# A prologue re-divided between TensorE and VectorE: half of each modulation sum, the transposes' eviction, the identity table's load and the rope angles

## What is computed

```python
cond = jax.nn.silu(c)                                  # 1024 values
mod = cond @ ada_w[i] + ada_b[i]                       # 1024 x 3072 for each layer
shift, scale, gate = jnp.split(mod, 3)
h = rms_norm_f32(x, norm_g[i]) * (1.0 + scale) + shift
out = retention_mixer(h, positions, ...)               # layer 0; q, k, v, g = split(h @ w_in)
x = x + gate * out
...
ang = positions[..., None] * inv_freq                  # in retention_mixer
cos, sin = jnp.cos(ang), jnp.sin(ang)
q = apply_rope(q, cos, sin); k = apply_rope(k, cos, sin) * RET_QK_DIM ** -0.5
```

## Time and profile before

| | |
|---|---|
| median of 3 runs | 2000.1 us (1998.48 to 2002.16) |
| the profiled execution: its time, its span | 1999.29 us, 1997.5 us |
| busy in the span: TensorE, VectorE, GpSimd, ScalarE | 1887.8 us (95%), 820.1 us (41%), 1104.3 us (55%), 458.1 us (23%) |
| mean granted TensorE clock, as a share of full speed | 0.968 |
| first of the projections' matmuls starts | 42.80 us |
| `tok` of tiles 4 and 5 starts | 66.91 us |

### The profile page before, as it was taken

The page is one execution under the profiler, slowest core; times in us unless marked ns, Lnnn a source line. Parts: engine busy times, 40 slices in busy tenths (PEclk is TensorE's granted clock), DMA queues, the critical chain, the costliest instruction groups (busy, mean ns, idle before and its releaser), DMA issues.

```text
span 1997.5 us, 27167 instructions
## 1 busy us (share of the span) xinstructions
PE 1887.8 (95%) x9662; PEld 1557.1 (78%) x9662; DVE 820.1 (41%) x1417; ACT 458.1 (23%) x933; POOL 1104.3 (55%) x856
## 2 busy tenths in 40 slices
PE   8999999998899999999998999989889869999998
PEld 4878888877788888888877778877768558887886
DVE  5642515444333432333322865975342553102300
ACT  3121111100222222222210246435122322001200
POOL 3755546486255444454456558752156468767862
PEclk9999999998899999999999998979899979999999
DMA  9423222265132222222223312110022133333331
GB/s 353 130 68 91 68 72 80 79 238 172 53 86 82 82 69 68 83 83 83 69 74 95 89 48 59 33 32 11 32 74 64 34 93 95 95 95 94 96 95 42
DMA packets 279466, 172.72 MB, mean 86 GB/s; under 512 B 5936, under 2 KB 269936, under 8 KB 278384
## 3 DMA queue, kind: packets, MB, share of 16 engines
q1 hardware_dynamic: 272912, 151.01, 26.0%
q10 hardware_dynamic: 6496, 20.93, 3.1%
HBM read 169.69 MB, written 2.10 MB: 86 GB/s over the span
## 4 chain that ended last, share of the span: by engine, by line
PE 83%; DVE 10%; ACT 2%; issue 2%; DMA 1%; POOL 1%; SPq 0%; DVEq 0%; ACTq 0%; POOLq 0%
PE acc L373 18%; PE acc L375 17%; PE acc L374 17%; PE acc L414 3%; PE acc L415 3%; PE acc L416 3%; PE st L427 3%; PE sc L1387 2%; PE ob L1332 2%; PE sc L1367 2%; DVE ada_acc L2069 2%; PE bc L460 2%; DVE conv_out L2192 2%; PE sc L1295 1%; DVE hn L508 1%
## 5 line engine op out<-in xcount | busy, mean ns | idle before, releaser
L711 POOL TENSOR_TENSOR wl<-raw,wh 128x512 fp32r<-128x512 f32 x464 | 651.8, 1426 | 19.4
L708 POOL TENSOR_SCALAR wh<-raw 128x1024 fp32r<-128x1024 f32 x232 | 258.0, 1112 | 724.0 <-PE acc L375 408.4
L373 PE MATMUL acc<-hh,wh 128*128 128x512 f32 x1056 | 430.5, 408 | 19.8 <-DVE hl L502 6.7
L375 PE MATMUL acc<-hh,wl 128*128 128x512 f32 x1056 | 417.3, 395 | 0.0
L374 PE MATMUL acc<-hl,wh 128*128 128x512 f32 x1056 | 416.5, 394 | 0.0
L373 PEld LDWEIGHTS acc<-hh,wh 128*128 128x128 f32 x1056 | 201.5, 191 | 69.6 <-issue 19.3
L375 PEld LDWEIGHTS acc<-hh,wl 128*128 128x128 f32 x1056 | 201.3, 191 | 43.5
L374 PEld LDWEIGHTS acc<-hl,wh 128*128 128x128 f32 x1056 | 202.2, 192 | 41.5 <-issue 2.2
L373 PE MATMUL acc<-Yh,wh 128*128 128x512 f32 x512 | 203.1, 397 | 5.5 <-DVE xT L577 5.5
L374 PE MATMUL acc<-Yl,wh 128*128 128x512 f32 x512 | 202.3, 395 | 0.0
L375 PE MATMUL acc<-Yh,wl 128*128 128x512 f32 x512 | 202.3, 395 | 0.0
(11 more groups left out here) (401 smaller groups left out, 2809.3 us busy)
## 6 DMA issues: line engine op xcount, KB each, us to landing
raw<-in_att_w_in SPq DMA_DIRECT2D x64, 512.0 KB, 4.0
raw<-in_mlp_w SPq DMA_DIRECT2D x64, 512.0 KB, 4.0
raw<-in_ret_w_in SPq DMA_DIRECT2D x48, 512.0 KB, 3.8
ada_w<-in_ada_w ACTq DMA_DIRECT2D x8, 1536.0 KB, 8.1
raw<-in_w_in SPq DMA_DIRECT2D x23, 512.0 KB, 3.7
ada_w<-in_ada_w SPq DMA_DIRECT2D x16, 512.0 KB, 10.7
raw<-in_ret_w_out SPq DMA_DIRECT2D x16, 512.0 KB, 4.0
raw<-in_att_w_out SPq DMA_DIRECT2D x16, 512.0 KB, 3.9
```

What stands on the lines that cost most here:

```text
L373: e.matmul(bank[:, :], wh[:, s, k, :], rhs_high(k), start=(start and k == 0), stop=False)
L375: last = e.matmul(bank[:, :], wl[:, s, k, :], rhs_high(k), start=False, stop=(stop and k == k1 - 1))
L708: e.tensor_scalar(wh[:, s, :, :], raw[:, s, :, :], 1.0, 1.0, ALU.mult, ALU.mult).then_inc(high_done, 1)
L711: low = e.tensor_tensor(wl[:, s, k0:k0 + KT // 2, :], raw[:, s, k0:k0 + KT // 2, :], wh[:, s, k0:k0 + KT // 2, :].bitcast(F32), ALU.subtract)
```

## The change

Four edits at the entry:

1. **Half of each block on VectorE.** `ada_half(n)` multiplies tiles 0 to 3 of block `n` with their value of `cond` and adds them up in `ada_acc0[:, n % 2, :]` (one TENSOR_SCALAR and three SCALAR_TENSOR_TENSOR over 128x512). TensorE multiplies tiles 4 to 7 as before and adds the partial sum over partitions by one more matmul with `ones`, which waits for `ada_half{n}` and stands in front of tile 6. So 5 matmuls for each block in place of 8.
2. **Transposes evicted by VectorE.** The eight evictions to `xT` move from ScalarE to VectorE as tensor copies.
3. **Identity table first.** The load of `const` moves from the second place of ScalarE's queue to the first of SyncE's, and the load of `pos` behind ScalarE's squares.
4. **Rope angles behind the norm.** The ten VectorE steps that make the angles move from the front of its program to behind the last `low`, ahead of the gate's partial sums; the two sines on ScalarE move behind its eight `hh`.

```diff
+        ada_acc0 = at("ada_acc0", [P, 2, S], W + 16 * KB)
...
+            e.dma_start(const[:, :], ins["const"]).then_inc(const_in, 16)
             for t in range(NT):
                 e.dma_start(x_tok[:, t, :], ins["x"][0, t * P:(t + 1) * P, :]).then_inc(x_in[t], 16)
...
-            e.dma_start(const[:, :], ins["const"]).then_inc(const_in, 16)
-            e.dma_start(pos[:, :], ins["positions"].to_broadcast([P, S])).then_inc(pos_in, 16)
...
-                x_out(t, 0)
-                x_out(t, 1)
+            e.dma_start(pos[:, :], ins["positions"].to_broadcast([P, S])).then_inc(pos_in, 16)
             e.dma_start(dec[:, :], ins["decay"][0]).then_inc(decay_in, 16)
             e.dma_start(glev[:, :, :], ins["levels"].rearrange("p (l n) -> p l n", l=LEVELS)).then_inc(levels_in, 16)
-            e.wait_ge(*V.at("angles"))
-            e.activation(sin_[:, :], ang[:, :], ACT.Sin).then_inc(*AC.done())
-            e.activation(cos_[:, :], tmp[:, 1, :], ACT.Sin).then_inc(*AC.done("rope"))
             e.wait_ge(*V.at("mod02"))
             for k in range(KT):
...
                 e.activation(hh[:, k, :], hn[:, k, :], ACT.Identity, bias=mod[:, 0, 0, k:k + 1]).then_inc(*AC.done(f"n0hi{k}"))
+            e.wait_ge(*V.at("angles"))
+            e.activation(sin_[:, :], ang[:, :], ACT.Sin).then_inc(*AC.done())
+            e.activation(cos_[:, :], tmp[:, 1, :], ACT.Sin).then_inc(*AC.done("rope"))
...
-                for k in range(KT):
+                for k in range(4, KT):
                     if k % 2 == 0:
                         e.wait_ge(ada_in[n][k // 2], 16)
+                    if k == 6:
+                        e.wait_ge(*V.at(f"ada_half{n}"))
+                        e.matmul(sc[n % 2][:, :], ones[:, :], ada_acc0[:, n % 2, :], start=False, stop=False)
                     last = e.matmul(sc[n % 2][:, :], cond[:, 0, k:k + 1].to_broadcast([P, P]), ada_w0[n][:, k, :],
-                                    start=(k == 0), stop=(k == KT - 1))
+                                    start=(k == 4), stop=(k == KT - 1))
...
+            for n in range(2 * NT):
+                e.wait_ge(*PE.at(f"x{n}"))
+                e.tensor_copy(xT[:, 4 * (n % 2):4 * (n % 2) + 4, n // 2 * P:(n // 2 + 1) * P],
+                              ob[n % 2][:, :].rearrange("p (k n) -> p k n", k=4)).then_inc(*V.done(f"x{n}"))
...
+            def ada_half(n):
+                if n >= 2:
+                    e.wait_ge(*PE.at(f"ada{n - 2}"))
+                for k in range(4):
+                    if k % 2 == 0:
+                        e.wait_ge(ada_in[n][k // 2], 16)
+                    x = ada_acc0[:, n % 2, :]
+                    if k == 0:
+                        step(e, e.tensor_scalar(x, ada_w0[n][:, 0, :], cond[:, 0, 0:1], None, ALU.mult), V)
+                    else:
+                        step(e, e.scalar_tensor_tensor(out=x, in0=ada_w0[n][:, k, :], scalar=cond[:, 0, k:k + 1], in1=x,
+                                                       op0=ALU.mult, op1=ALU.add), V, f"ada_half{n}" if k == 3 else None)
...
+            ada_half(0)
             ada_part(0)
-            e.wait_ge(*AC.at(f"x{2 * NT - 1}"))
             e.wait_ge(*PE.at("n0bc"))
+            ada_half(1)
             for k in range(4):
                 normed(k)
             ada_part(1)
+            ada_half(2)
             for k in range(4, KT):
                 normed(k)
             ada_part(2)
+            ada_half(3)
             for k in range(4):
                 low(k)
             ada_part(3)
             for k in range(4, KT):
                 low(k)
+            e.wait_ge(pos_in, 16)
+            step(e, e.tensor_copy(ang[:, :], pos[:, :]), V)
...
+            step(e, e.tensor_scalar(tmp[:, 1, :], tmp[:, 1, :], -1.0, TURN / 4, ALU.mult, ALU.add), V, "angles")
+
             for k in range(KT):
                 e.wait_ge(gate_in[k], 16)
                 gate_sum(e, k)
```

More of the change, by code:

```diff
@@ L794, in _ @@
             e.dma_start(small[:, :], ins["small"]).then_inc(small_in, 16)
-            e.dma_start(const[:, :], ins["const"]).then_inc(const_in, 16)
-            e.dma_start(pos[:, :], ins["positions"].to_broadcast([P, S])).then_inc(pos_in, 16)
             e.wait_ge(small_in, 16)
             e.activation(cond[:, 1, :], sm("c"), ACT.Tanh, scale=0.5).then_inc(*AC.done("cond_tanh"))
-            def x_out(t, half):
-                n = 2 * t + half
-                e.wait_ge(*PE.at(f"x{n}"))
-                e.activation(xT[:, 4 * half:4 * half + 4, t * P:(t + 1) * P],
-                             ob[half][:, :].rearrange("p (k n) -> p k n", k=4), ACT.Copy).then_inc(*AC.done(f"x{n}"))
             for t in range(NT):
@@ L1282, in _ @@
                     if t >= 1:
-                        e.wait_ge(*AC.at(f"x{2 * t + half - 2}"))
+                        e.wait_ge(*V.at(f"x{2 * t + half - 2}"))
                     for k in range(4):
@@ L1948, in gains @@
                                                in1=sm(f"norm_g{layer}"), op0=ALU.add, op1=ALU.mult), V)
-            e.wait_ge(pos_in, 16)
-            step(e, e.tensor_copy(ang[:, :], pos[:, :]), V)
-            step(e, e.tensor_scalar(ang[:, :], ang[:, :], sm("inv_freq"), None, ALU.mult), V)
-            step(e, e.tensor_scalar(tmp[:, 0, :], ang[:, :], 1.0 / TURN, ROUND, ALU.mult, ALU.add), V)
-            step(e, e.tensor_scalar(tmp[:, 0, :], tmp[:, 0, :], -ROUND, None, ALU.add), V)
-            for part in TURN_PARTS:
-                step(e, e.scalar_tensor_tensor(out=ang[:, :], in0=tmp[:, 0, :], scalar=-part, in1=ang[:, :],
-                                               op0=ALU.mult, op1=ALU.add), V)
-            step(e, e.tensor_scalar(ang[:, :], ang[:, :], PI_BELOW, -PI_BELOW, ALU.min, ALU.max), V)
-            step(e, e.scalar_tensor_tensor(out=tmp[:, 1, :], in0=ang[:, :], scalar=-1.0, in1=ang[:, :],
-                                           op0=ALU.mult, op1=ALU.max), V)
-            step(e, e.tensor_scalar(tmp[:, 1, :], tmp[:, 1, :], -1.0, TURN / 4, ALU.mult, ALU.add), V, "angles")
+            for n in range(2 * NT):
+                e.wait_ge(*PE.at(f"x{n}"))
+                e.tensor_copy(xT[:, 4 * (n % 2):4 * (n % 2) + 4, n // 2 * P:(n // 2 + 1) * P],
+                              ob[n % 2][:, :].rearrange("p (k n) -> p k n", k=4)).then_inc(*V.done(f"x{n}"))
             e.wait_ge(*AC.at(f"n0ss{NT - 1}"))
@@ L2004, in _ @@
                 low(k)
+            e.wait_ge(pos_in, 16)
+            step(e, e.tensor_copy(ang[:, :], pos[:, :]), V)
+            step(e, e.tensor_scalar(ang[:, :], ang[:, :], sm("inv_freq"), None, ALU.mult), V)
+            step(e, e.tensor_scalar(tmp[:, 0, :], ang[:, :], 1.0 / TURN, ROUND, ALU.mult, ALU.add), V)
+            step(e, e.tensor_scalar(tmp[:, 0, :], tmp[:, 0, :], -ROUND, None, ALU.add), V)
+            for part in TURN_PARTS:
+                step(e, e.scalar_tensor_tensor(out=ang[:, :], in0=tmp[:, 0, :], scalar=-part, in1=ang[:, :],
+                                               op0=ALU.mult, op1=ALU.add), V)
+            step(e, e.tensor_scalar(ang[:, :], ang[:, :], PI_BELOW, -PI_BELOW, ALU.min, ALU.max), V)
+            step(e, e.scalar_tensor_tensor(out=tmp[:, 1, :], in0=ang[:, :], scalar=-1.0, in1=ang[:, :],
+                                           op0=ALU.mult, op1=ALU.max), V)
+            step(e, e.tensor_scalar(tmp[:, 1, :], tmp[:, 1, :], -1.0, TURN / 4, ALU.mult, ALU.add), V, "angles")
             for k in range(KT):
```

## The result

The changed kernel has a median of 2009.18 us over 12 runs (2002.53 to 2014.38), the kernel before 1998.87 over 12 runs beside it (1994.27 to 2003.96). The ratio is 1.0048, 95% interval 1.0036 to 1.006, so it is slower by 9.6 us (1998.87 x 0.0048); the medians lie 10.3 us apart. The profiled execution took 2009.03 us with a span of 2007.4, 9.9 more than the span before.

The account below looks back on a forecast made before the run. VectorE's uncovered halves 2 and 3, the count at `low(4)` and the late eviction were taken to delay `tok` by 9.5 us: 1999.3 + 9.5 + 0.8 = 2009.6 us, range 2004 to 2015.

Parts of the forecast that it names:

- half 2: VectorE's half sum for block 2, behind `ada_part(1)`: 2.6 us, starting at 33.4 and ending at 36.1.
- `low(0..3)`: First group of four `low` steps on VectorE: 3.52 us plus 1.3 beside a GpSimd split, ending at 49.1.
- clock loss in `pair`: TensorE's `pair`, behind a 5.4 us wait, runs at the lower clock at first: 1.5 us added.
- VectorE's chain: Halves 2 and 3 have no idle time to cover them, so later VectorE steps shift; half 3 ends at 44.3.
- the count at `low(4)`: Ten angle steps ending VectorE's prologue make `pair` wait for `low(4)`: start at 52.3, 9.5 us later than 42.80.
- the used-up slack: TensorE's 1.7 us wait ahead of `tok` for the splits of tiles 4 and 5 is eaten; `tok` starts about 76.4.
- rival 3: The forecast plus the low clock through the whole entry, in TensorE's gaps between blocks: 2015 us; chance 0.13.
- The eviction arrives with TensorE: Ahead of `feat` of tile 2: q's first-half eviction ends at 63.7 and `pair` at 63.6, both paths arriving together.
- The table load: On ScalarE between the sines and q's eviction: 1.28 us, with the skill's further 1.38 us of draining left out.
- Rival 4: Each VectorE step beside a split waits for a whole GpSimd instruction: 5.6 us more, 2015.2 us; chance 0.05.
- rival 2: TensorE's saved 10.3 us come through, if landings are not what holds it: 1989.8 us; chance 0.03.
- The last step of the sum: At the entry's end: TensorE arrives at 76.2, and `tok` was put at about 76.4.

Follow-up runs that it names:

- e5: Kernel before with the half sums alone (edit 1; angles at the front, evictions on ScalarE, loads as before): ratio 1.0068 to the kernel before.
- e3: As e2, with ten counted one-column memsets on VectorE behind the last `low`: ratio 1.0069 to the kernel before, median 2014.02 us.
- e2: Changed kernel with angles behind half 0 and sines ahead of `hh`, half sums kept: ratio 1.0038 to the kernel before, median 2006.82 us.
- e1: Changed kernel with the ten angle steps counted on the gate sums' counter instead of VectorE's: ratio 1.007 to the kernel before.
- e10: As e1, with idle TensorE matmuls added ahead of the `ones` matmuls of blocks 2 and 3: ratio 1.0061 to the kernel before.
- e6: Kernel before with the gate's eight loads moved behind weight tiles 4 and 5 in SyncE's queue: ratio 0.9981 to the kernel before.

## Why the prediction held, step by step

Forecast 2009.6, measured 2009.18. The steps:

| step | forecast | measured |
|---|---|---|
| `ada_part(1)` starts | 29.65 | 28.14 |
| half 2, its end | 2.6 us, 36.1 | 4.6 us, 35.1 |
| `ada_part(2)` starts | 38.8 | 38.09 |
| half 3, its end | 3.9 us, 44.3 | 4.4 us, 44.1 |
| `low(0..3)`, end | 4.82 us, 49.1 | 6.42 us, 50.6 |
| block 3 on TensorE done | 46.9 | 49.7 |
| `low(4)` ends, `pair` starts | 52.3 (+9.5) | 53.76 (+10.9) |
| angles end | 60.6 | 61.3 |
| ScalarE ready for q's eviction | 63.1 | 63.8 |
| clock loss in `pair` | 1.5 | 1.1 |
| `feat` starts | 65.2 | 66.17 |
| splits of 4 and 5 | 11.4 us, 75.1 | 12.2 us, 77.3 |
| `tok` starts | 76.4 (+9.5) | 77.45 (+10.5) |

- **The place and the mechanism held.** VectorE's chain, the count at `low(4)` and the used-up slack are each there in the profile; e5 shows the first without the other edits, e3 the second without the late eviction, and the 15.15 us for which GpSimd waited for TensorE the third. How the 10.5 us divide among them is not measured: the halves alone (e5) cost more than all four edits. That TensorE's three matmuls less for each block count for nothing was right too: TensorE waits 9.4 us for the sums that replace them.
- **Two terms were too small.** `low(0..3)` was put at 4.82, the row of a group beside one split; here it stands beside two and took 6.42. A half sum was put at 2.6 us from other VectorE steps over 128x512 and takes 2.86 with nothing beside it. Half 2 was taken as undisturbed; it ran beside the split of tile 1 (30.31 to 33) and took 4.6. The second was made good: `ada_part(1)` started 1.5 us earlier, as TensorE has less to do in block 1 (done at 28.1 and not 29.5, for which I had allowed nothing), and it took 2.3 us in place of 3.8, so that half 2 began at 30.46 where I had 33.4.
- **The clock was put in the wrong place.** I gave it 1.5 us in `pair`, where it took 1.1 (12.41 against 11.32), and by rival 3 a little in the gaps. It also slowed block 3 (done at 49.7 and not 46.9), which is hidden as VectorE is with `low` until 50.6. Rival 3 in its full size isn't there in this profile. The clock was at its lower level in several gaps of e2, e3 and e5 (0.50 or 0.51 in four-microsecond stretches), so its condition does occur in this program; how much of their late `tok` it makes isn't separated. The changed kernel's two slowest executions, 2014.38 and 2014.37 us, have the lowest mean granted clocks of its twelve, 0.961 and 0.962; they were not traced.
- **The eviction arrives with TensorE**, as forecast: ScalarE was 1.23 us ahead. e1 and e10 show how thin that is: with `pair` 2.1 and 1.5 us earlier and the sines 2.5 and 3.1 us later, `feat` waits 3.9 us.
- **The table load.** In e1 the eviction starts at 66.33, 0.01 us behind the load of 65.04 + 1.28, with TensorE's data long there, and likewise in e10 (66.90 behind 65.61 + 1.28). The 1.38 us of draining that the Trainium skill, "ScalarE: Activation LUTs", section "What ACT_TABLE_LOAD costs", adds to it is not seen in these rows, and the sum was right to leave it out.
- **Rival 4** (each VectorE step beside a split waits for a whole GpSimd instruction) would have made half 3 9.5 us long. It took 4.4, at most 6.4 in the experiments. By the rule of the Trainium skill, "SBUF — State Buffer", section "SBUF: two separate sides", it would be 9.5 by the prediction's estimate; the rows lie between that and no contention at all (2.86).
- **The argument against rival 2** (the landing of tile 4 holds `tok`) held in e6, but with less behind it than I wrote: the slot of the ring frees only 2.6 us before the landing.

- **The last step of the sum**, from 76.2 to 76.4, had no row behind it; TensorE came at 77.2 and waited 0.24 us for the split.

That the median fits to half a microsecond is partly luck. The forecast stands on 2000.1 us for the kernel before, which took 1998.87 beside the changed one: +9.5 us were forecast, and the medians give +10.3, the profiled executions +9.7. In the profile `tok` was off by 1.0, the rest of the span by 0.6 the other way, and one execution differs from the next by more.

## What to carry to other kernels

Before work is moved from the busiest engine to an idle-looking one, look at the second engine's idle time in that very stretch, and at what stands beside it: a half sum cost 2.86 us alone and up to 6.4 beside GpSimd's splits. When steps that signal a counter are added at the end of a prologue, check every wait that is resolved by counting back from that end; ten steps of no weight made a wait of 3.3 us here and, with the lower clock behind it, 5.2 us. And behind a wait that is removed, look for the next two: here they were a late eviction and a slot of the ring, 1 to 3 us away. A profile is one execution: before a difference of a few microseconds is read from it, look at its granted clock and at where it stands among the others.

## What the hardware showed that I had not expected

- The granted clock differs between executions of one kernel (0.961 to 0.969 on average in the changed kernel's twelve), and at the entry it feeds back through VectorE. With gaps of 3.10 and 3.36 us ahead of block 2, e1 was granted 0.50 in 32:36, and the changed kernel 1.00 all through 29.4:42.8. At the low clock e1's block 2 ended later, so half 3 fell beside more of a split, so block 3 waited 6.97 us rather than 4.49.

```profile
32.00:36.00 4.00, 3.99 (x5) 1.24 (x5) 3.89 (x5) 0.00 (x0) 1.08 (x1) 0.50 1.05 387
```

- The same four VectorE steps over 128x512 took 2.86, 4.6, 4.4, 5.4, 6.2 and 6.4 us, depending on the split beside them, and GpSimd's two steps in turn 2.5 us alone and up to 4.37 beside VectorE. Both engines slow each other down; neither price is a constant.
